# The low halves of the MLPs' turned activations are subtracted by GpSimd, on a semaphore of their own, in place of VectorE

## The chip, the cores and the metric

The kernel runs on one core of one Trainium2 chip. The metric is the time of one execution on the device in microseconds; three runs before the change took 2456.23 to 2458.35, median 2457.49. Durations and starts below come from one profiled execution of that kernel.

Engines by their short names: PE is TensorE (PEld its weight loads), ACT is ScalarE, DVE is VectorE, POOL is GpSimd, SP is SyncE.

## The reference

A trunk of two layers over 256 tokens of width 2048, all in float32: a Mamba-2 mixer and an MLP, then a differential attention over one shared key/value set and a second MLP. What matters here is the MLP, which stands in both layers:

```
h = h + sq_relu_mlp(rms_norm(h, mlp_norm_w[l]), w_up[l], w_down[l])
def sq_relu_mlp(h, w_up, w_down):
    return jnp.square(jax.nn.relu(h @ w_up)) @ w_down      # 2048 -> 8192 -> 2048
```

## The kernel before

**Products in three parts.** A float32 product is made of three matmuls on rounded values: every factor is split into a high half (the value rounded to TensorE's format) and a low half (value minus high half), and TensorE adds high times high, high times low and low times high. ScalarE makes the high halves (a copy that rounds), VectorE the low ones (a subtraction).

**Weights.** They stream from DRAM in pieces of 128x1024 elements (512 KB), 865 of them, through rings of four slots: `raw` (loaded by SyncE), `whi` (ScalarE, `hi`, L741), `wlo` (VectorE, `lo`, L1095). TensorE uses a piece in 12 matmuls (`piece`, L422 to L424) and then raises `w_used`, for which ScalarE's piece four further on waits. So ScalarE and VectorE can be at most four pieces ahead of TensorE. Each engine has its program written out by hand: a loop over the pieces, and at given piece numbers `j`, behind the weight work of this piece, other work.

**An MLP** (`mlp` on each engine) is four chunks of 64 pieces. In a chunk, pieces 0 to 31 multiply by the up weights and give four blocks of 512 hidden columns (u = 0 to 3) in PSUM; pieces 32 to 63 multiply these by the down weights. The second product needs the hidden activations with channels on the partitions, split into halves. For block u this takes:
- `relu` on ScalarE and `square` on VectorE (L1380), then a VectorE transpose within 32x32 squares (`turn`, L1336), which raises `turned`;
- `spread(n)` on GpSimd's queue: one write to DRAM (L1673) and four reads back (L1678) into `channel_tiles`, of which there are two, used by turns. n numbers all blocks that are turned in this way, the MLPs' and the residual stream's: the first MLP's blocks have n = 5 to 20, the second's 29 to 44;
- `up_hi` on ScalarE (L932): waits for the four reads, writes the high half into `st` and raises `turned_hi`;
- `up_lo` on VectorE (L1387): waits for `turned_hi`, writes the low half and raises `turned_lo`.

TensorE waits for `turned_lo` at the first uses of each block among the down pieces (from piece 32 on; block 3 from piece 44). `spread(n)` waits for the low half of block n - 2 before it overwrites that channel tile. The residual stream's blocks go the same way with `resid_hi` and `resid_lo`, and raise the same `turned_lo`.

**Where it stands in the stream.** Tables give, for each block, the last piece of its product, the piece at which it is read (relu, square, transpose, GpSimd's trip) and the piece at which its halves are made. `UPS` holds for the second to fourth chunk, `UPS_FIRST` for the first chunk of each MLP, where blocks 0 and 1 take turns and so end two pieces apart:

```
UPS = ((0, 7, 11, 18), (1, 15, 19, 26), (2, 23, 27, 34), (3, 31, 35, 42))
UPS_FIRST = ((0, 13, 17, 24), (1, 15, 19, 27), (2, 23, 27, 34), (3, 31, 35, 42))
```

At piece 27 of a first chunk ScalarE's order is: high half of the weight piece, `up_hi` of block 1, `relu` of block 2, and then the high half of piece 28. VectorE's is: low half of piece 27, `up_lo` of block 1, square and transpose of block 2, low half of piece 28.

GpSimd has little else in the MLPs: it goes through `spread(n)` for n = 1, 2, 3 ... in order.

Of the kernel before, what the change touches and what calls it, by code (L numbers as in the profile page):

```python
# [17 lines left out]
F32 = mybir.dt.float32  # L18
F32R = mybir.dt.float32r
ALU = mybir.AluOpType  # L20
# [36 lines left out]
T_OUT, T_MLP0, T_MLP0_END, T_WO, T_MLP1 = 0, 4, 20, 24, 28  # L57
# [47 lines left out]
class Chain:  # L105
# [25 lines left out]
    def leave(self, rounds):  # L131
        assert self.n == self.per, (self.n, self.per)
        self.base, self.n = 0, self.before + rounds * self.per


def wait(eng, sem, n):
    if not (isinstance(n, int) and n <= 0):
        eng.wait_ge(sem, n)
# [24 lines left out]
def trunk(nc, x, mlp_norm_w, w_up, w_down, ssm_norm_w, ssm_w_in, ssm_conv_w, ssm_conv_b, ssm_dt_bias,  # L163
# [3 lines left out]
    with ctx:  # L167
# [5 lines left out]
        def sem(name):  # L173
            if name not in sems:
                sems[name] = ctx.enter_context(nc.semaphore(name))
            return sems[name]
# [4 lines left out]
        st = sb("stationary", [P, 3 * KT, 2, SEQ], F32R)  # L181
        RA, RB, RC = 0, KT, 2 * KT
# [104 lines left out]
        channel_tiles = [b.rearrange("p (b k i) -> p k b i", k=4, i=32) for b in channels]  # L287
# [109 lines left out]
        def _(pe):  # L397
# [191 lines left out]
            def mlp(base, R, T, U):  # L589

                def up(c, fresh):
                    for i, (u, kt) in enumerate(WO_ORDER if fresh else PLAIN):
                        if kt == 0:
                            pe.wait_ge(sem("resid_added"), R + 4 * c + u - 3 if c else R if u >= 2 else R - 1)
                        if fresh and u == 0 and kt % 4 == 0:
                            pe.wait_ge(sem("turned_lo"), T - 3 + kt // 4)
                        piece(Pos(base, c, PER_CHUNK), i, banks[u], NB, RA + kt, kt == 0, kt == KT - 2)

                def down(c):
                    for i, (d, kt) in enumerate(WO_ORDER):  # L600
                        if kt == 0:
                            pe.wait_ge(sem("up_read"), c * 4 + (U + d + 1))
                        if d == 0 and kt % 4 == 0:
                            pe.wait_ge(sem("turned_lo"), c * 4 + (T + 1 + kt // 4))
                        if base == UP1 and c == 3 and i == 31:
                            last_piece(Pos(base, c, PER_CHUNK), 32 + i, banks[d], RB + kt)
                        else:
                            piece(Pos(base, c, PER_CHUNK), 32 + i, banks[d], NB, RB + kt, kt == 0, kt == KT - 2)

                for c in range(4):  # L610
                    up(c, c == 0)
                    down(c)
# [48 lines left out]
            def pair(j, first):  # L661
                pos = Pos(ATT0, j, PER_PAIR)
                for i in range(PER_PAIR):
                    m, kt = LATE_ORDER[i] if first else (i // 8, 2 * (i % 8))
                    if first:
                        if i == 0:
                            pe.wait_ge(sem("resid_added"), R_WO - 1)
                        if m == 0 and kt == 12:
                            pe.wait_ge(sem("kv_lo"), 1)
                        elif m == 0 and kt % 4 == 0 or m == 2 and kt == 12:  # L670
                            pe.wait_ge(sem("turned_lo"), T_MLP0_END + 1 + kt // 4)
                    else:
                        if i == 0:
                            wait(pe, sem("o_lo"), j - 1)
                        if i == 8:
                            pe.wait_ge(sem("k_read"), j)
                        if i == 16:
                            pe.wait_ge(sem("q_read"), j)
                    ps, region = ((aux[0], RA), (acc[0], RA), (acc[1], RC))[m]
                    piece(pos, i, ps, NB, region + kt, kt == 0, kt == KT - 2)  # L680
                    if not first:
                        if i == 4:
                            turn_q(j - 1)
                        if i == 7:
                            scores_a(j - 1)
                        if i == 9:
                            pe.wait_ge(sem("v_read"), j + 1)
                            scores_b(j - 1)
                        if i == 15:
                            turn_p(j - 1)  # L690
                        if i == 16:
                            apply_p(j - 1)
                        if i == 20:
                            turn_o(j - 1)
# [393 lines left out]
        def _(v):  # L1088
# [287 lines left out]
            def mlp(base, R, T, U, T_carry, before, after, prev, squared):  # L1376
                def square(c, u):

                    v.wait_ge(sem("relu_made"), c * 4 + (U + u + 1))
                    v.scalar_tensor_tensor(act, banks[u][:, :, :], 0.0, act, ALU.max, ALU.mult).then_inc(sem("up_read"), 1)  # L1380
                    v.wait_ge(sem("up_read"), c * 4 + (U + u + 1))
                    turn(act, c * 4 + (T + u + 1), (T + u + 1) % 2)

                def up_lo(c, u):
                    v.wait_ge(sem("turned_hi"), c * 4 + (T + u + 1))
                    hi, lo = (st[:, RB + 4 * u:RB + 4 * u + 4, i, :].rearrange("p k (b i) -> p k b i", i=32) for i in range(2))
                    v.tensor_tensor(lo, channel_tiles[(T + u + 1) % 2], hi.bitcast(F32), ALU.subtract).then_inc(sem("turned_lo"), 1)  # L1387

                def chunk(c, first, carry):
                    for j in range(PER_CHUNK):  # L1390
                        lo(Pos(base, c, PER_CHUNK), j)
                        if first:
                            if j == 2:
                                resid_lo(2, T - 1, before)
                            if j == 3:
                                prev()
                                turn_resid(3, R, T)
                            if j == 10:
                                resid_lo(3, T, before)
                            if j == 9:  # L1400

                                link(resid_ms(squared))
                                link(v.reciprocal(h_rs, h_ms))
                        elif j == 3:
                            add_resid(3, Pos(base, c, PER_CHUNK), -1, True, banks[3])
                        for u, last, at_read, at_lo in UPS_FIRST if first else UPS:
                            if j == at_read:
                                square(c, u)
                            if j == at_lo:
                                up_lo(c, u)  # L1410
                        for d, last, at_add, at_lo in DOWNS:
                            if j == at_add:
                                add_resid(d, Pos(base, c, PER_CHUNK), last, True, banks[d])
                                if carry:
                                    turn_resid(d, R + 13 + d, T_carry + d + 1)
                            if j == at_lo and carry:
                                resid_lo(d, T_carry + d + 1, after)

                chunk(0, True, False)
                with v.Fori(1, 3) as c:  # L1420
                    chunk(c, False, False)
                chunk(3, False, after is not None)
# [140 lines left out]
        def _(gp):  # L1563
# [104 lines left out]
            def spread(n):  # L1668

                gp.wait_ge(sem("turned"), n)  # L1670
                wait(gp, sem("spread"), (n - 2) * 64)
                scratch = spread_dram[n % 2]
                gp.dma_start(scratch.rearrange("t b c q f -> (b c) t (q f)"),  # L1673
                             squares_t[n % 2].rearrange("p (t f) -> p t f", t=TT)).then_inc(sem("spread_out"), 16)
                gp.wait_ge(sem("spread_out"), n * 16)
                wait(gp, sem("turned_lo"), n - 2)
                for q in range(4):
                    gp.dma_start(channels[n % 2][32 * q:32 * q + 32, :].rearrange("c (b f) -> c b f", f=P),  # L1678
                                 scratch[:, :, :, q, :].rearrange("t b c f -> c (t b) f")).then_inc(sem("spread"), 16)


            gp.wait_ge(sem("resid_added"), 1)
# [5 lines left out]
            gp.wait_ge(sem("masks_made"), 1)  # L1688
            for n in range(1, T_WO + 1):
                spread(n)  # L1690
            gp.wait_ge(sem("h_ms"), 1)
            rsqrt(h_rs, h_ms, "h_rstd")

# [25 lines left out]
            rsqrt(o_rs, o_ss, "o_rstd")  # L1719
            for n in range(T_WO + 1, T_MLP1 + 16 + 1):  # L1720
                spread(n)


# [20 lines left out]
```

## Time and profile before

| | |
|---|---|
| runs, us | 2456.23, 2457.49, 2458.35 |
| span of the profiled execution, us | 2456.4 |
| TensorE busy | 2441.9 us, 99% |
| VectorE busy | 1539.9 us, 63% |
| ScalarE busy | 1195.5 us, 49% |
| GpSimd busy | 259.1 us, 11% |
| chain that ended last | TensorE 99%, DMA 1% |
| granted TensorE clock | 9 tenths or more in all 40 slices |

The profiled execution's own time is not listed apart from its span; the median of the runs is 1.1 us above it. Busy shares are averages over the span. In a timeline a row gives the start, the length, the engine, the line and the operation, then how long the engine had been idle and who ended that.

### The profile page before, as it was taken

Reading aid. Unit: us, or ns where it says so; the run is one execution under the profiler, and the core shown is the slowest. Engines: PE = TensorE matmul, PEld = TensorE weight load, DVE = VectorE, ACT = ScalarE, POOL = GpSimd, SP = SyncE. Lnnn points to the kernel's source line nnn. Section 1 sums busy time; section 2 is a strip of 40 time slices with the busy share of each in tenths; the row PEclk is TensorE's granted clock in tenths of the full one; section 3 lists DMA queues with packets and bytes.
Section 4 is the critical chain, followed back from the end, with each engine's and each line's share of the span. In section 5 each row is a group of like instructions: output and inputs, shape, how many; then the busy total and the mean of one; then the engine's idle time right before and its main releaser. Section 6 shows DMA issues by size and latency. Waiting matters only on the chain.

```text
span 2456.4 us, 32498 instructions
## 1 busy us (share of the span) xinstructions
PE 2441.9 (99%) x11683; PEld 2039.3 (83%) x11683; DVE 1539.9 (63%) x1664; ACT 1195.5 (49%) x1442; POOL 259.1 (11%) x394
## 2 busy tenths in 40 slices
PE   8999999999999999999999999999999999999999
PEld 7888888888888888888888888888888888888887
DVE  5788888875565555565555766666655565565554
ACT  5556555654444344344444545555544444444443
POOL 1011111111011000010011111110110010010010
PEclk9999999999999999999999999999999999999999
DMA  7777777777678677677687766655886686786785
GB/s 205 225 225 228 230 223 228 224 222 238 216 230 241 193 228 230 191 233 223 193 245 238 235 202 194 187 176 175 262 244 213 204 237 207 210 240 197 219 237 169
DMA packets 288103, 535.30 MB, mean 218 GB/s; under 512 B 22318, under 2 KB 55440, under 8 KB 286976
## 3 DMA queue, kind: packets, MB, share of 16 engines
q1 hardware_dynamic: 264736, 457.87, 61.3%
q0 software_dynamic: 22976, 75.91, 11.2%
q8 instruction: 69, 1.13, 0.2%
q14 instruction: 34, 0.28, 0.0%
q10 hardware_dynamic: 288, 0.11, 0.0%
HBM read 498.09 MB, written 35.72 MB: 217 GB/s over the span
## 4 chain that ended last, share of the span: by engine, by line
PE 99%; DMA 1%; DVE 0%; ACT 0%; SPq 0%; issue 0%; ACTq 0%
PE acc L422 18%; PE acc L424 18%; PE acc L423 18%; PE aux L424 12%; PE aux L423 12%; PE aux L422 12%; PE aux L438 1%; PE aux L439 1%; PE aux L437 1%; PE aux L510 1%; PE aux L452 1%; DMA resid<-in_x 1%; PE acc L504 0%; PE aux L653 0%; PE aux L654 0%; PE aux L560 0%
## 5 line engine op out<-in xcount | busy, mean ns | idle before, releaser
L1095 DVE TENSOR_TENSOR w_lo<-w_raw,w_hi 128x1024 fp32r<-128x1024 f32 x865 | 1053.5, 1222 | 824.6 <-ACT w_hi L741 824.0
L741 ACT ACTIVATE w_hi<-w_raw 128x1024 fp32r<-128x1024 f32 x865 | 913.2, 1060 | 1076.9 <-PE acc L424 545.6
L422 PE MATMUL acc<-w_hi,stationary 128*128 128x512 f32 x1984 | 778.5, 392 | 0.0
L424 PE MATMUL acc<-w_hi,stationary 128*128 128x512 f32 x1984 | 773.2, 390 | 0.0
L423 PE MATMUL acc<-w_lo,stationary 128*128 128x512 f32 x1984 | 773.0, 390 | 0.0
L422 PE MATMUL aux<-w_hi,stationary 128*128 128x512 f32 x1340 | 522.1, 390 | 0.0
L424 PE MATMUL aux<-w_hi,stationary 128*128 128x512 f32 x1340 | 521.9, 389 | 0.0
L423 PE MATMUL aux<-w_lo,stationary 128*128 128x512 f32 x1340 | 521.8, 389 | 0.0
L424 PEld LDWEIGHTS acc<-w_hi,stationary 128*128 128x128 f32 x1984 | 372.5, 188 | 77.9
L422 PEld LDWEIGHTS acc<-w_hi,stationary 128*128 128x128 f32 x1984 | 372.6, 188 | 76.4
L423 PEld LDWEIGHTS acc<-w_lo,stationary 128*128 128x128 f32 x1984 | 372.7, 188 | 75.9
L423 PEld LDWEIGHTS aux<-w_lo,stationary 128*128 128x128 f32 x1340 | 251.6, 188 | 52.2
L424 PEld LDWEIGHTS aux<-w_hi,stationary 128*128 128x128 f32 x1340 | 251.6, 188 | 52.1
L422 PEld LDWEIGHTS aux<-w_hi,stationary 128*128 128x128 f32 x1340 | 251.6, 188 | 52.0
L1673 POOL DMA_DIRECT2D spread<-work x44 | 31.8, 723 | 1179.4 <-DVE work L1336 971.9
L1678 POOL DMA_DIRECT2D work<-spread x176 | 102.2, 587 | 169.0 <-DMA spread<-work 164.0
L1575 POOL TENSOR_TENSOR small<-small 128x2 f32<-128x2 f32 (+2 forms) x22 | 43.9, 2001 | 391.7 <-DVE small L1105 391.7
L437 PE MATMUL aux<-stationary,w_hi 128*128 128x256 f32 x256 | 72.6, 284 | 0.0
L439 PE MATMUL aux<-stationary,w_hi 128*128 128x256 f32 x256 | 72.6, 283 | 0.0
L438 PE MATMUL aux<-stationary,w_lo 128*128 128x256 f32 x256 | 72.5, 283 | 0.0
L437 PEld LDWEIGHTS aux<-stationary,w_hi 128*128 128x128 f32 x256 | 49.2, 192 | 0.3
L438 PEld LDWEIGHTS aux<-stationary,w_lo 128*128 128x128 f32 x256 | 49.1, 192 | 0.3
(206 smaller groups left out, 1170.3 us busy)
## 6 DMA issues: line engine op xcount, KB each, us to landing
w_raw<-in_w_up SPq DMA_DIRECT2D x256, 512.0 KB
w_raw<-in_w_down SPq DMA_DIRECT2D x256, 512.0 KB
w_raw<-in_ssm_w_in SPq DMA_DIRECT2D x129, 512.0 KB
w_raw<-in_ssm_w_out SPq DMA_DIRECT2D x64, 512.0 KB
w_raw<-in_w_kv SPq DMA_DIRECT2D x64, 512.0 KB
spread<-work POOLq DMA_DIRECT2D x44, 512.0 KB, 3.8
work<-spread POOLq DMA_DIRECT2D x176, 128.0 KB, 5.0
w_raw<-in_ssm_w_in SPq DMA_DIRECT2D x64, 256.0 KB
```

What stands on the lines that cost most here:

```text
L422: pe.matmul(o, xh, hi[:, k], start=start, stop=False)
L423: pe.matmul(o, xh, lo[:, k], start=False, stop=False)
L424: mm = pe.matmul(o, xl, hi[:, k], start=False, stop=stop)
L437: pe.matmul(o, hi[:, k, i], xh, start=start, stop=False)
L438: pe.matmul(o, lo[:, k, i], xh, start=False, stop=False)
L439: mm = pe.matmul(o, hi[:, k, i], xl, start=False, stop=stop)
L452: tr = pe.transpose(dst(i, t), src(i, t), ident[:, :])
L741: a.activation(whi[:, s, :], raw[:, s, :], ACT.Copy).then_inc(sem("hi_made"), 1)
L1095: v.tensor_tensor(wlo[:, s, :], raw[:, s, :], whi[:, s, :].bitcast(F32), ALU.subtract).then_inc(sem("lo_made"), 1)
L1575: gp.tensor_tensor(out, in_, nhalf[:, 0:out.shape[1]], ALU.pow).then_inc(sem(signal), 1)
L1673: gp.dma_start(scratch.rearrange("t b c q f -> (b c) t (q f)"), squares_t[n % 2].rearrange("p (t f) -> p t f", t=TT)).then_inc(sem("spread ...
L1678: gp.dma_start(channels[n % 2][32 * q:32 * q + 32, :].rearrange("c (b f) -> c b f", f=P), scratch[:, :, :, q, :].rearrange("t b c f -> c ( ...
```

## The change

The subtraction `up_lo` leaves VectorE's program and comes into GpSimd's, with the same operands and shape. It stands behind `spread(n)` for each n that is a block of an MLP, and waits there for `turned_hi`. It raises a new semaphore, `up_lo`, for which TensorE waits in the down product. `turned_lo` now counts the residual's blocks alone, and the numbers waited for are converted by two small functions. Before a channel tile is overwritten, `spread` waits for whichever of the two semaphores belongs to block n - 2.

```diff
+def is_up(n):
+    return T_MLP0 < n <= T_MLP0_END or n > T_MLP1
+def resid_block(n):
+    return n if n <= T_MLP0 else n - 16
+def up_block(n):
+    return n - T_MLP0 if n <= T_MLP0_END else n - T_MLP1 + 16
...
                         if d == 0 and kt % 4 == 0:
-                            pe.wait_ge(sem("turned_lo"), c * 4 + (T + 1 + kt // 4))
+                            pe.wait_ge(sem("up_lo"), c * 4 + (U + 1 + kt // 4))
...
-                def up_lo(c, u):
-                    v.wait_ge(sem("turned_hi"), c * 4 + (T + u + 1))
-                    hi, lo = (st[:, RB + 4 * u:RB + 4 * u + 4, i, :].rearrange("p k (b i) -> p k b i", i=32) for i in range(2))
-                    v.tensor_tensor(lo, channel_tiles[(T + u + 1) % 2], hi.bitcast(F32), ALU.subtract).then_inc(sem("turned_lo"), 1)
...
-                            if j == at_lo:
-                                up_lo(c, u)
...
                 gp.wait_ge(sem("spread_out"), n * 16)
-                wait(gp, sem("turned_lo"), n - 2)
+                if is_up(n - 2):
+                    gp.wait_ge(sem("up_lo"), up_block(n - 2))
+                else:
+                    wait(gp, sem("turned_lo"), resid_block(n - 2))
...
+            def up_lo(n):
+                u = (up_block(n) - 1) % 4
+                hi, lo = (st[:, RB + 4 * u:RB + 4 * u + 4, i, :].rearrange("p k (b i) -> p k b i", i=32) for i in range(2))
+                gp.wait_ge(sem("turned_hi"), n)
+                gp.tensor_tensor(lo, channel_tiles[n % 2], hi.bitcast(F32), ALU.subtract).then_inc(sem("up_lo"), 1)
...
             for n in range(1, T_WO + 1):
                 spread(n)
+                if is_up(n):
+                    up_lo(n)
```

The order on GpSimd at blocks 0 and 1 of the first MLP's first chunk, before: a write and four reads for each block.

```order
L1673 DMA spread<-work 128x2x512 [waits spread,turned]
L1678 DMA work<-spread 32x8x128 [waits turned_lo,spread_out]
L1678 DMA work<-spread 32x8x128 x3
L1673 DMA spread<-work 128x2x512 [waits spread,turned]
L1678 DMA work<-spread 32x8x128 [waits turned_lo,spread_out]
```

And the same place in the changed kernel, whose lines are numbered anew (L1681 is the write, L1689 the reads, L1697 the subtraction):

```order
L1681 DMA spread<-work 128x2x512 [waits spread,turned]
L1689 DMA work<-spread 32x8x128 [waits turned_lo,spread_out]
L1689 DMA work<-spread 32x8x128 x3
L1697 TENSOR_TENSOR stationary<-work,stationary 128x4x256 [waits turned_hi]
L1681 DMA spread<-work 128x2x512 [waits spread,turned]
L1689 DMA work<-spread 32x8x128 [waits turned_lo,spread_out]
```

Between the last read of a block and the write of the next there now stands an operation that waits for ScalarE's `turned_hi`.

VectorE from the transpose of block 1 to that of block 2 in the same chunk, before (L1380 is the square, L1336 the transpose, L1095 the low half of a weight piece, L1387 the subtraction):

```order
L1336 STREAM_TRANSPOSE work<-work 128x2x4x4x32 [waits spread_out,up_read]
L1095 TENSOR_TENSOR w_lo<-w_raw,w_hi 128x1024 [waits hi_made] x5
L1387 TENSOR_TENSOR stationary<-work,stationary 128x4x256 [waits turned_hi]
L1095 TENSOR_TENSOR w_lo<-w_raw,w_hi 128x1024 [waits hi_made] x3
L1387 TENSOR_TENSOR stationary<-work,stationary 128x4x256 [waits turned_hi]
L1380 SCALAR_TENSOR_TENSOR work<-aux,work 128x1024 [waits relu_made]
L1336 STREAM_TRANSPOSE work<-work 128x2x4x4x32 [waits spread_out,up_read]
```

And in the changed kernel:

```order
L1351 STREAM_TRANSPOSE work<-work 128x2x4x4x32 [waits spread_out,up_read]
L1110 TENSOR_TENSOR w_lo<-w_raw,w_hi 128x1024 [waits hi_made] x8
L1395 SCALAR_TENSOR_TENSOR work<-aux,work 128x1024 [waits relu_made]
L1351 STREAM_TRANSPOSE work<-work 128x2x4x4x32 [waits spread_out,up_read]
L1110 TENSOR_TENSOR w_lo<-w_raw,w_hi 128x1024 [waits hi_made] x8
```

The two subtractions are gone from between the weight pieces; the rest stands as it stood. The orders of ScalarE and TensorE have the same instructions at the same places.

## Rows read from the trace of the kernel before

**Rows 1.** The page: busy time by engine, and the chain that ended last.
```profile
PE 2441.9 (99%) x11683; PEld 2039.3 (83%) x11683; DVE 1539.9 (63%) x1664; ACT 1195.5 (49%) x1442; POOL 259.1 (11%) x394
...
PE 99%; DMA 1%; DVE 0%; ACT 0%; SPq 0%; issue 0%; ACTq 0%
```

**Rows 2.** Timeline of TensorE at the start: start, length, engine, operation, idle before.
```profile
15.09 1.97 PE L452 MATMUL aux<-ident,resid 128*128 128x128 f32 x8 [6.41 <-DMA resid<-in_x]
...
19.79 0.28 PE L473 MATMUL acc<-stationary,w_hi 128*64 128x256 f32 x1
```

**Rows 3.** Timeline of VectorE, first MLP, first chunk, pieces 24 and 28.
```profile
739.07 1.23 DVE L1095 TENSOR_TENSOR w_lo<-w_raw,w_hi 128x1024 fp32r<-128x1024 f32 x1 [1.49 <-ACT w_hi L741]
...
749.50 1.22 DVE L1380 SCALAR_TENSOR_TENSOR work<-aux,work 128x1024 f32<-128x1024 f32 x1
750.76 1.25 DVE L1336 STREAM_TRANSPOSE work<-work 128x1024 f32<-128x1024 f32 x1
751.93 2.32 DVE L1095 TENSOR_TENSOR w_lo<-w_raw,w_hi 128x1024 fp32r<-128x1024 f32 x2
```

**Rows 4.** Timeline of ScalarE there: high halves of blocks 0, 1, relu of 2.
```profile
738.94 1.04 ACT L932 ACTIVATE stationary<-work 128x1024 fp32r<-128x1024 f32 x1
...
747.10 1.04 ACT L932 ACTIVATE stationary<-work 128x1024 fp32r<-128x1024 f32 x1
748.05 1.00 ACT L928 ACTIVATE work<-aux 128x1024 f32<-128x1024 f32 x1
```

**Rows 5.** Timeline of TensorE: first matmuls of pieces 27 and 28.
```profile
754.03 0.39 PE L422 MATMUL aux<-w_hi,stationary 128*128 128x512 f32 x1
...
756.75 0.39 PE L422 MATMUL aux<-w_hi,stationary 128*128 128x512 f32 x1
```

**Rows 6.** Groups by line and shape: busy time, mean ns, idle before.
```profile
L1387 DVE TENSOR_TENSOR stationary<-work,stationary 128x1024 fp32r<-128x1024 f32 x32 | 39.0, 1219 | 2.2 <-ACT stationary L932 2.2
...
L1568 POOL TENSOR_SCALAR_AFFINE_SELECT work<-work 128x256 f32<-128x256 f32 x8 | 7.0, 876 | 9.9 <-ACT work L860 9.9
```

**Rows 7.** Timeline of VectorE and GpSimd in the mixer, from 128 us.
```profile
128.15 2.29 DVE L1304 TENSOR_TENSOR work<-work,colv 128x2048 f32<-128x2048 f32 x1
...
128.33 2.68 POOL L1575 TENSOR_TENSOR small<-small 128x2 f32<-128x2 f32 x1 [14.39 <-DVE small L1105]
```

**Rows 8.** Timeline, first MLP, second chunk: ScalarE's block 0, GpSimd's block 1.
```profile
896.64 1.05 ACT L932 ACTIVATE stationary<-work 128x1024 fp32r<-128x1024 f32 x1
...
903.52 0.72 POOL L1673 DMA_DIRECT2D spread<-work  x1 [15.52 <-DVE work L1336]
```

**Rows 9.** Timeline of GpSimd, first chunk: write of block 1, trip of block 2.
```profile
730.27 0.72 POOL L1673 DMA_DIRECT2D spread<-work  x1
...
752.30 0.72 POOL L1673 DMA_DIRECT2D spread<-work  x1 [12.64 <-DVE work L1336]
756.36 2.33 POOL L1678 DMA_DIRECT2D work<-spread  x4 [3.34 <-DMA spread<-work]
```

**Rows 10.** L1678's landings for the four copies from 727.96, 1367.52 and 1855.66.
```profile
DMA to landing us min/median/max: 3.7/3.8/5.4
...
DMA to landing us min/median/max: 3.2/3.3/3.6
...
DMA to landing us min/median/max: 4.1/4.8/7.9
```

**Rows 11.** Timeline of GpSimd and ScalarE, second MLP, first chunk, block 3.
```profile
1855.66 2.32 POOL L1678 DMA_DIRECT2D work<-spread  x4 [5.35 <-DMA spread<-work]
...
1865.30 1.06 ACT L932 ACTIVATE stationary<-work 128x1024 fp32r<-128x1024 f32 x1 [1.23 <-DMA work<-spread]
```

**Rows 12.** Timeline of ScalarE, second MLP, first chunk: high halves of blocks 0, 1.
```profile
1815.01 1.04 ACT L932 ACTIVATE stationary<-work 128x1024 fp32r<-128x1024 f32 x1
...
1823.17 1.05 ACT L932 ACTIVATE stationary<-work 128x1024 fp32r<-128x1024 f32 x1
```

**Rows 13.** The chain in order of time: eight later transposes.
```profile
70.52 0.87 PE aux L452 x8
```

More of the change, by code:

```diff
@@ L595, in up @@
                         if fresh and u == 0 and kt % 4 == 0:
-                            pe.wait_ge(sem("turned_lo"), T - 3 + kt // 4)
+                            pe.wait_ge(sem("turned_lo"), resid_block(T - 3) + kt // 4)
                         piece(Pos(base, c, PER_CHUNK), i, banks[u], NB, RA + kt, kt == 0, kt == KT - 2)
@@ L670, in pair @@
                         elif m == 0 and kt % 4 == 0 or m == 2 and kt == 12:
-                            pe.wait_ge(sem("turned_lo"), T_MLP0_END + 1 + kt // 4)
+                            pe.wait_ge(sem("turned_lo"), resid_block(T_MLP0_END + 1) + kt // 4)
                     else:
@@ L1721, in _ @@
                 spread(n)
+                if is_up(n):
+                    up_lo(n)
 _INS = ["x", "mlp_norm_w", "w_up", "w_down", "ssm_norm_w", "ssm_w_in", "ssm_conv_w", "ssm_conv_b", "ssm_dt_bias",
```

## The prediction

> **What bounds the kernel now.** I read the page first. TensorE is busy for 2441.9 of 2456.4 us, the chain that ended last is TensorE for 99%, and the other engines have room: VectorE 63%, ScalarE 49%, GpSimd 11% [rows 1]. TensorE's one long wait lies at the start, 6.41 us for the input [rows 2]. So work taken from VectorE can give nothing by itself: no matmul waits for it. What can move the time is a wait that the change creates and that reaches TensorE. For that I read the timelines of ScalarE, VectorE, GpSimd and TensorE side by side, where the subtractions stand.
>
> The pipeline: each weight piece goes ScalarE (high half, L741), VectorE (low half, L1095), TensorE (12 matmuls; piece 27 starts at 754.03 and piece 28 at 756.75, so 2.72 us a piece [rows 5]). The ring has four slots, so the halves of a piece are ready well before use. Piece 24 of the first MLP's first chunk had its low half at 739.07 + 1.23 = 740.30 [rows 3], and was begun four pieces before 756.75, at 745.87: a cover of 5.6 us. Piece 28 is the tight one. Behind piece 27 ScalarE makes the high half of block 1 (747.10) and the relu of block 2 (748.05) [rows 4]; VectorE then squares, transposes (749.50, 750.76) and only then makes the low half of piece 28, 751.93 + 1.16 = 753.1 [rows 3]. TensorE wants it at 756.75 [rows 5]. The cover there is 3.65 us.
>
> **The change part by part.**
> (a) Removed: 32 VectorE subtractions of 1219 ns, 39.0 us [rows 6]. Worth nothing, since what hides them is the matmul stream itself (99%). The one place where it shortens a path is just behind ScalarE's op at 747.10: the square no longer stands behind the subtraction and can follow the relu at once, 0.4 us earlier than now.
> (b) Added: 32 GpSimd subtractions of the same size. The trace has none on this engine. Lower bound: what VectorE needs, 1.2 us. Upper bound: GpSimd's AFFINE_SELECT over a quarter of the elements took 876 ns, so four times that, 3.5 us [rows 6]. The two ends are far apart and neither row is nearer in kind (one has the operation, the other the engine), so I take the middle, 2.4 us. The Trainium skill (GPSIMD Engine Reference, "3.1 Elementwise — side-by-side cycle accounting") gives 4497 ns for a two-input fp32 operation of 2048 elements, so an estimate of 2.25 us for 1024; no run here shows it yet, and by it each stall below would be 0.15 us shorter.
> (c) GpSimd's operation may wait for VectorE. At 128.33 a GpSimd operation on two columns took 2.68 us, just as long as it took until 0.57 us behind the end of a VectorE operation of 2.29 us with two inputs in SBUF, begun 0.18 us before it [rows 7]. In the first chunk ScalarE's block ends at 738.94 + 1.04 = 739.98 while the subtraction of piece 24 runs until 740.30 [rows 3, 4]: I start GpSimd at 740.3. The Trainium skill (SBUF — State Buffer, "Who interferes with whom") says that a VectorE instruction with two SBUF inputs and a GpSimd instruction that reads SBUF exclude each other for the whole instruction; the trace agrees so far (2.68 us). It speaks against the change: by it each of the 32 also holds up a weight subtraction by up to its own length. With no exclusion GpSimd would start 0.3 us earlier. Held up by 2.4 us, a weight subtraction stays inside the 5.6 us of cover, so this costs nothing more.
> (d) Moved, and this decides: the subtraction sits in GpSimd's single stream between one block's four copies back and the next block's trip through DRAM. GpSimd waits in it for the high half of block n; queued behind it are the next block's one write and four reads, then the next subtraction; for them ScalarE waits, and behind ScalarE the weight pieces. In an ordinary chunk that is free: the high half ends at 896.64 + 1.05 = 897.7, and the next trip starts at 903.52 anyway [rows 8], so the subtraction has 5.8 us. In the first chunk of each MLP it is not: blocks 0 and 1 are ready two pieces apart, so block 1's trip was issued at 730.27 [rows 9], 8.7 us before block 0's high half even began.
>
> The sum for that place:
> - subtraction 740.3 to 742.7; the trip of block 1 issued at 742.75 in place of 730.27.
> - first copy back 4.06 us later (752.30 to 756.36 [rows 9]), at 746.8; the fourth follows after three issues of 0.58, at 748.55 (four take 2.32).
> - the fourth copy is the last to land. Of three trips the slowest copy landed after 5.4, 3.6 and 7.9 us [rows 10]; that of the third is the fourth copy (1855.66 + 1.74 + 7.9 = 1865.30, where ScalarE had waited for it [rows 11]). I take 6.2, somewhat above the middle of the ends, since the weight loads compete until the ring is full and then stop. It lands at 754.75 instead of in time for 747.10.
> - from there the chain of (ScalarE block 0.95, relu 1.00, hand-over 0.1, square 1.26, transpose 1.17, low half of piece 28 1.16) is 5.65 us: ready at 760.4.
> - needed at 756.75: TensorE stands still for 3.65 us.
>
> The second MLP has the same spacing: high halves at 1815.01 and 1823.17, 8.16 us apart, as 738.94 and 747.10 [rows 4, 12]. So two stalls, 7.3 us. Block 2's trip then starts near 759.5 in place of 752.30 and would hold ScalarE some 2 us more at piece 34, but there is no relu behind it and the 5.6 us of cover hold. The low halves themselves are used from piece 32 on (767.6) and are done by 742.7; the last is wanted at piece 44, some 8 us behind its end. Everything later shifts with TensorE.
>
> The span becomes 2456.4 + 7.3 = 2463.7 us. The median of the runs shown, 2457.49, lies 1.1 us above that span, so I add it: 2464.8, given as 2465.
>
> **The rivals.**
> 1. Not slower: the copies land fast enough. The mechanism is the same trip, with a subtraction of 1.2 us and a last landing of 3.6 us [rows 6, 10]: issued at 741.55, last copy begun at 747.35, landed at 750.95, piece 28 ready at 756.6, just before 756.75. It decides from there: subtraction and landing together up to 5.0 us. For it: when ScalarE stops, the ring fills and the weight loads stop too, which leaves the queues to these copies. Against it: only one of the three rows is that short. The time is then 2457.5; a half-way form (landing 4.5, subtraction 2.2) gives 1.75 us a stall and 2461.
> 2. The stalls also cost clock. After the idle 6.41 us at the start, eight transposes took 1.97 us where eight later ones took 0.87, and the slow pace ended by the matmul at 19.79 [rows 2, 13]. That is the lower of the two levels, 1.2 GHz, for 4.7 us of work, 2.3 us lost. For it: a standstill of 3.65 us. Against: the shown idle was nearly twice as long, and the granted clock is 2.4 GHz in all 40 slices of the page. It would give 2465 + 2 x 2.3 = 2469.5.
> 3. A GpSimd subtraction much longer than its upper bound: from 5.8 us on it also delays the trips of the 24 ordinary blocks. Against: the longest GpSimd operation among the rows, held up for most of it, is 2.68 us [rows 7]. At 6 us the two stalls are 7.25 us each, so 2472.
> 4. The change does not do what it says: faster, because VectorE's 39 us come back. The chain has no VectorE share for it to come back from.
>
> **How the numbers follow.** Forecast 0.52, rival 1 0.24, rival 2 0.16, rival 3 0.07, rival 4 0.01. The ends of the unknown costs: 1.2 and 3.6 give no stall, 2457.5; 3.5 and 7.9 give 3.65 + 1.1 + 1.7 = 6.45 each, 2470.4, and with the clock 2475. The range 2457.5 to 2472 leaves out the upper corner of rivals 2 and 3. The forecast's own range, with landings from 5 to 7.5, is 2461 to 2469. About 0.2%, 4.9 us, is what a measurement of this kernel tells from no change, so a stall must be above 2.45 us to count: that holds for most of the forecast, for rivals 2 and 3, and for little of rival 1. Slower 0.70, same 0.28, faster 0.02.
>
> **What would show it.** In the new profile: TensorE waits for the low half (w_lo) twice, once in each MLP, 27 to 28 pieces into its first chunk, 2 to 5 us each, and ScalarE waits just before it for a DMA of work from spread, about 7 us. The write of block 1 is issued right behind the GpSimd subtraction, some 4 us after the start of ScalarE's block 0 in place of 8.7 us before it. In ordinary chunks the writes start when the transposes end, as now, and nobody waits. If TensorE waits nowhere, the landing was the wrong term; if it waits in every chunk, the length of the subtraction was.

## The result, and the profile after

| | before | changed |
|---|---|---|
| median of 5 runs, us | 2457.39 | 2465.79 |
| lowest to highest | 2456.18 to 2458.35 | 2463.84 to 2468.64 |
| ratio (95% interval) | | 1.0038 (1.0026 to 1.0051) |
| span of the profiled execution | 2456.4 | 2465.7 |

The change makes the kernel slower by 0.38% by the ratio; the medians lie 8.4 us apart, 0.34%. A time of 2465 was predicted, 7.3 us of it loss. The profiled execution of the changed kernel took 1.7 us more than the median of its runs, so the two spans lie 9.3 us apart and not 8.4. In what follows a trip is the write of one block to DRAM and its four copies back, and a landing is the time from the issue of a copy to its arrival.

The page of the changed kernel, busy time and the chain that ended last (before: [rows 1]):

```profile
PE 2443.9 (99%) x11683; PEld 2038.8 (83%) x11683; DVE 1527.4 (62%) x1632; ACT 1194.4 (48%) x1442; POOL 338.5 (14%) x426
...
PE 87%; issue 6%; DMA 3%; DVE 2%; ACT 1%; POOL 1%; SPq 0%; DVEq 0%; ACTq 0%; POOLq 0%
```

TensorE's busy time hardly moves, but the chain now leaves it. GpSimd gained 79.4 us. VectorE lost only 12.5 of the 39.0 us taken from it. Groups of instructions by line say why (busy time, mean ns, idle before): the weight subtractions before and after, and GpSimd's new operation (VectorE's before: [rows 6]):

```profile
L1095 DVE TENSOR_TENSOR w_lo<-w_raw,w_hi 128x1024 fp32r<-128x1024 f32 x865 | 1053.5, 1222 | 824.6 <-ACT w_hi L741 824.0
```
```profile
L1110 DVE TENSOR_TENSOR w_lo<-w_raw,w_hi 128x1024 fp32r<-128x1024 f32 x865 | 1076.7, 1251 | 833.5 <-ACT w_hi L756 832.6
```
```profile
L1697 POOL TENSOR_TENSOR stationary<-work,stationary 128x1024 fp32r<-128x1024 f32 x32 | 79.0, 2468 | 284.3 <-ACT stationary L947 284.3
```

One subtraction takes 2468 ns on GpSimd against 1219 on VectorE, and the weight subtractions grew by 23.2 us in all; the 3.3 us that are left of the 26.5 lie in VectorE's other lines. The one that meets the first GpSimd subtraction is in VectorE's timeline below with 1.87 us.

TensorE's waits, in total (waited for, times, longest):

```profile
PE aux L437 <- DVE w_lo L1110: 7.8, 2, 4.8
```

Two waits for a weight's low half that were not there. They stand where they were expected, and the timelines show how they come about. First MLP, GpSimd (before: [rows 9]):

```profile
739.52 2.50 POOL L1697 TENSOR_TENSOR stationary<-work,stationary 128x1024 fp32r<-128x1024 f32 x1 [9.82 <-ACT stationary L947]
741.98 0.73 POOL L1681 DMA_DIRECT2D spread<-work  x1
745.73 2.33 POOL L1689 DMA_DIRECT2D work<-spread  x4 [3.02 <-DMA spread<-work]
```

ScalarE (before: [rows 4]):

```profile
738.39 1.05 ACT L947 ACTIVATE stationary<-work 128x1024 fp32r<-128x1024 f32 x1
...
753.68 1.06 ACT L947 ACTIVATE stationary<-work 128x1024 fp32r<-128x1024 f32 x1 [7.04 <-DMA work<-spread]
```

VectorE and TensorE (before: [rows 3, 5]):

```profile
741.24 1.87 DVE L1110 TENSOR_TENSOR w_lo<-w_raw,w_hi 128x1024 fp32r<-128x1024 f32 x1 [1.50 <-ACT w_hi L756]
...
758.11 4.59 DVE L1110 TENSOR_TENSOR w_lo<-w_raw,w_hi 128x1024 fp32r<-128x1024 f32 x4
```
```profile
759.35 0.50 PE L437 MATMUL aux<-w_hi,stationary 128*128 128x512 f32 x1 [2.98 <-DVE w_lo L1110]
```

Read downwards: GpSimd idle for 9.82 us until the high half of block 0 is there; its subtraction; the write of block 1 right behind; the copies; ScalarE idle for 7.04 us; the four low halves made in a burst once it goes on; TensorE idle for 2.98 us. In the second MLP the same happens with larger numbers, and a new one. GpSimd and ScalarE:

```profile
1821.38 0.73 POOL L1681 DMA_DIRECT2D spread<-work  x1
1826.95 2.33 POOL L1689 DMA_DIRECT2D work<-spread  x4 [4.85 <-DMA spread<-work]
```
```profile
1834.94 1.06 ACT L947 ACTIVATE stationary<-work 128x1024 fp32r<-128x1024 f32 x1 [8.89 <-DMA work<-spread]
```

TensorE there, the stretch behind its wait, and for comparison the stretch behind the wait of the first MLP (columns of the second and third fence: stretch, length, busy time with count of PE, PEld, DVE, ACT and POOL, granted clock, DMA share, GB/s):

```profile
1840.61 0.79 PE L437 MATMUL aux<-w_hi,stationary 128*128 128x512 f32 x1 [4.83 <-DVE w_lo L1110]
...
1842.06 0.63 PE L437 MATMUL aux<-w_hi,stationary 128*128 128x512 f32 x1
1842.48 0.63 PE L438 MATMUL aux<-w_lo,stationary 128*128 128x512 f32 x1
```
```profile
1840.60:1843.30 2.70, 2.69 (x6) 2.15 (x7) 2.70 (x3) 0.09 (x1) 0.00 (x0) 0.50 0.84 227
```
```profile
759.30:763.00 3.70, 3.65 (x16) 2.99 (x17) 3.40 (x3) 0.13 (x1) 0.43 (x1) 1.00 0.87 237
```

The write took 5.57 us to the first copy here, 3.75 in the first MLP, although it was issued at the same place between two weight loads both times (SyncE issued the next load at 743.13 and at 1822.55, 1.15 and 1.17 us behind the write). And behind this wait the clock was granted at 0.50, its level of 1.2 GHz: six matmuls follow each other at 0.43 us and more in place of 0.227 (2.72 us for the 12 of a piece), which costs about 1.4 us. Behind the first wait it stayed at 2.4 GHz.

Stalls of 7.8 and clock of 1.4 make 9.2 of the 9.3 us between the two spans. The agreement to 0.1 us is partly chance: before the first stall this execution was 0.55 us ahead of the other (ScalarE's block 0 at 738.39 against 738.94).

An ordinary chunk is as it was (before: [rows 8]): the subtraction ends at 903.03, the next write starts at 906.93 when VectorE has turned the block.

```profile
900.54 2.49 POOL L1697 TENSOR_TENSOR stationary<-work,stationary 128x1024 fp32r<-128x1024 f32 x1 [9.71 <-ACT stationary L947]
906.93 0.73 POOL L1681 DMA_DIRECT2D spread<-work  x1 [3.90 <-DVE work L1351]
```

### The profile page after: what moved, and what is told of

Same layout as the page of the kernel before. It is cut to its first block, busy times and chain, and to the rows that moved or that the text cites. A ratio compares the mean times of both kernels' runs of the same rounds, so it can differ in the third digit from the quotient of the medians.

```text
span 2465.7 us, 32482 instructions
## 1 busy us (share of the span) xinstructions
PE 2443.9 (99%) x11683; PEld 2038.8 (83%) x11683; DVE 1527.4 (62%) x1632; ACT 1194.4 (48%) x1442; POOL 338.5 (14%) x426
## 4 chain that ended last, share of the span: by engine, by line
PE 87%; issue 6%; DMA 3%; DVE 2%; ACT 1%; POOL 1%; SPq 0%; DVEq 0%; ACTq 0%; POOLq 0%
PE acc L437 16%; PE acc L439 16%; PE acc L438 16%; PE aux L437 11%; PE aux L439 11%; PE aux L438 11%; DMA spread<-work 1%; PE aux L453 1%; PE aux L454 1%; PE aux L452 1%; DVE w_lo L1110 1%; DMA work<-back 1%; PE aux L525 1%; PE aux L467 1%; POOL work L1689 0%
## 5 line engine op out<-in xcount | busy, mean ns | idle before, releaser
L1110 DVE TENSOR_TENSOR w_lo<-w_raw,w_hi 128x1024 fp32r<-128x1024 f32 x865 | 1076.7, 1251 | 833.5 <-ACT w_hi L756 832.6
L1681 POOL DMA_DIRECT2D spread<-work x44 | 32.0, 727 | 845.2 <-DVE work L1351 661.2
L1689 POOL DMA_DIRECT2D work<-spread x176 | 102.4, 588 | 162.0 <-DMA spread<-work 157.0
L1697 POOL TENSOR_TENSOR stationary<-work,stationary 128x1024 fp32r<-128x1024 f32 x32 | 79.0, 2468 | 284.3 <-ACT stationary L947 284.3
```

What stands on the lines that cost most here:

```text
L1110: v.tensor_tensor(wlo[:, s, :], raw[:, s, :], whi[:, s, :].bitcast(F32), ALU.subtract).then_inc(sem("lo_made"), 1)
L1697: gp.tensor_tensor(lo, channel_tiles[n % 2], hi.bitcast(F32), ALU.subtract).then_inc(sem("up_lo"), 1)
```

## The experiments

All are compared with runs of the kernel before on the same chip: experiments 1 to 4 with one set of them (median 2457.70), 5 to 8 with another (2457.42), 9 with a third (2458.04).

| kernel | median us | ratio to before (95%) |
|---|---|---|
| 1 trip of block 1 first | 2457.42 | 1.0000 (0.9991 to 1.0009) |
| 2 bare wait | 2465.70 | 1.0030 (1.0018 to 1.0042) |
| 3 GpSimd in ordinary chunks only | 2458.41 | 1.0001 (0.9992 to 1.0010) |
| 4 GpSimd in first chunks only | 2467.01 | 1.0040 (1.0027 to 1.0054) |
| 5 subtraction made twice | 2475.59 | 1.0074 (1.0060 to 1.0087) |
| 6 halves of block 1 at piece 30 | 2465.90 | 1.0037 (1.0023 to 1.0051) |
| 7 bare wait, light loads | 2457.56 | 1.0003 (0.9994 to 1.0012) |
| 8 changed kernel, light loads | 2461.29 | 1.0016 (1.0007 to 1.0025) |
| 9 halves at 30, and block 2's trip first | 2457.41 | 1.0000 (0.9991 to 1.0009) |

**1. The trip of block 1 ahead of the subtraction of block 0.**

```diff
+FIRST_BLOCKS = (T_MLP0 + 1, T_MLP1 + 1)
                 spread(n)
-                if is_up(n):
+                if is_up(n) and n not in FIRST_BLOCKS:
+                    if n - 1 in FIRST_BLOCKS:
+                        up_lo(n - 1)
                     up_lo(n)
```

> The changed kernel with one thing moved: in the first chunk of each MLP, GpSimd makes the trip of block 1 before it subtracts block 0 (then both subtractions, then block 2); all 32 subtractions stay on GpSimd. Theory A (GpSimd's order: the trip of block 1 stands behind a wait for block 0's high half): both stalls of TensorE vanish, 2457.5 us, ratio 1.000 within 0.001, and ScalarE waits for no copy at piece 27. Rival B (GpSimd's subtractions themselves cost, by holding up VectorE's weight subtractions through the SBUF port): the time stays near 2465, since the same 32 subtractions run. Rival C (block 2's trip, now behind two subtractions, becomes the late one): a smaller stall at piece 34, 2459 to 2461.

Measured: ratio 1.0000, TensorE waits for nothing but its input. GpSimd:

```profile
740.09 2.50 POOL L1700 TENSOR_TENSOR stationary<-work,stationary 128x1024 fp32r<-128x1024 f32 x1 [1.60 <-ACT stationary L950]
747.33 2.52 POOL L1700 TENSOR_TENSOR stationary<-work,stationary 128x1024 fp32r<-128x1024 f32 x1 [4.73 <-ACT stationary L950]
751.00 0.73 POOL L1684 DMA_DIRECT2D spread<-work  x1 [1.16 <-DVE work L1354]
```

All 32 subtractions run on GpSimd at the same 2.5 us, and the weight subtractions take 1251 ns in the mean here too: the whole loss was the order at one place per MLP. Rivals B and C fall.

**2. The bare wait.** VectorE subtracts as before; GpSimd only waits.

```diff
                 spread(n)
+                if T_MLP0 < n <= T_MLP0_END:        # and n > T_MLP1 in the second loop
+                    gp.wait_ge(sem("turned_hi"), n)
```

> The kernel before, with VectorE's subtractions where they were, and a bare wait of GpSimd for the block's high half behind each trip. Theory A (it is the place in the queue): the trip of block 1 is issued at about 739.9 to 740.1 in place of 742.0 in the changed kernel, so each stall is about 2.5 us shorter, less 0.4 us for the subtraction that stands again before the square: 1 us in the first MLP, 1 to 3 in the second, 2459 to 2461.5. Rival B (the cost is GpSimd's operation): no stall, 2457.5.

Measured: 2465.70, above the expected range. Rival B falls, but the size is off: in time the wait alone costs as much as wait and subtraction. GpSimd and ScalarE, first MLP:

```profile
739.68 0.72 POOL L1673 DMA_DIRECT2D spread<-work  x1 [10.00 <-ACT stationary L932]
746.00 2.33 POOL L1678 DMA_DIRECT2D work<-spread  x4 [5.60 <-DMA spread<-work]
```
```profile
753.91 1.06 ACT L932 ACTIVATE stationary<-work 128x1024 fp32r<-128x1024 f32 x1 [7.32 <-DMA work<-spread]
```

The write started 2.3 us earlier than in the changed kernel, and its first copy 0.3 us later: 6.32 us in place of 3.75. The stalls were 3.49 and 2.53 us, 6.0 in place of the 7.8 of the changed kernel, and the clock was at its lower level behind both: 13 matmuls at 0.43 us and more in the first MLP, 8 in the second, where the fall came 1.5 us after TensorE had started again. That costs about 2.8 and 1.6 us, 4.4 in all. So the loss has another make-up than in the changed kernel: less standstill, more clock. The profiled execution took 4.1 us more than the median of its runs, so the median run had less of one or the other. (A third wait, of 0.78 us at 1394.83, lies outside the MLPs.) What lengthened the write is the question of experiments 7 and 8.

**3 and 4. The two halves of the change.** In 3, VectorE makes the eight subtractions of the first chunks and GpSimd the other 24; in 4 it is the other way round. The edit in 3 (in 4 both conditions are turned over):

```diff
+                            if j == at_lo and first:
+                                up_lo(c, u)                # VectorE, raising up_lo
...
-                if is_up(n):
+                if is_up(n) and not in_first(n):
                     up_lo(n)                               # GpSimd
```

> GpSimd subtracts only the 24 blocks of the second to fourth chunks; the 8 blocks of the two first chunks are VectorE's again (on the same new semaphore). Theory A: no stall, 2457.5 us, ratio 1.000 within 0.001, although 24 operations of 2.5 us run on GpSimd and delay weight subtractions by up to 2.5 us. Rival B (exclusion through the port costs in proportion): three quarters of the loss, 2463.7.

> The complement: GpSimd subtracts only the 8 blocks of the two first chunks, VectorE the other 24. Theory A: the whole loss, 2464 to 2467. Rival B: a quarter of it, 2459.5.

Measured: 1.0001 and 1.0040. The loss is wholly in the first chunks. With 24 subtractions on GpSimd the weight subtractions took 1246 ns in the mean in place of 1222, and no loss came of it that these runs tell apart. The profiled execution of experiment 4 is the fastest of its five runs (2464.23): stalls of 2.04 and 3.38 us, and no fall of the clock.

**5. The subtraction made twice.**

```diff
+                link(gp.tensor_tensor(lo, channel_tiles[n % 2], hi.bitcast(F32), ALU.subtract))
                 gp.tensor_tensor(lo, channel_tiles[n % 2], hi.bitcast(F32), ALU.subtract).then_inc(sem("up_lo"), 1)
```

> The changed kernel with each GpSimd subtraction made twice, one behind the other, so that about 5.0 us stand where 2.5 us stood. Theory A (order on GpSimd): the trip of block 1 in each first chunk is issued 2.5 us later, each stall is 2.5 us longer, plus 1.3 us in the first MLP too if the clock falls there as it did in the second MLP of the changed kernel: 2470.5 to 2473. Ordinary chunks stay free, since 5.0 is under the 5.8 us they have. Rival (proportional cost of the exclusion): the loss doubles, 2474.

Measured: 2475.59, above the expected range. GpSimd and TensorE, first MLP:

```profile
742.24 3.27 POOL L1698 TENSOR_TENSOR stationary<-work,stationary 128x1024 fp32r<-128x1024 f32 x1
745.47 0.73 POOL L1681 DMA_DIRECT2D spread<-work  x1
```
```profile
762.52 0.80 PE L437 MATMUL aux<-w_hi,stationary 128*128 128x512 f32 x1 [6.02 <-DVE w_lo L1110]
763.12 0.63 PE L438 MATMUL aux<-w_lo,stationary 128*128 128x512 f32 x1
```

The second subtraction took 3.27 us beside a weight subtraction that had started to wait at 741.38 and ended at 743.24, 1.07 us behind the end of GpSimd's first. Where VectorE had nothing waiting, the second took no longer than the first:

```profile
756.58 2.36 POOL L1697 TENSOR_TENSOR stationary<-work,stationary 128x1024 fp32r<-128x1024 f32 x1 [5.02 <-ACT stationary L947]
759.02 2.36 POOL L1698 TENSOR_TENSOR stationary<-work,stationary 128x1024 fp32r<-128x1024 f32 x1
```

So the trip of block 1 was issued 3.3 to 3.4 us later than in the changed kernel, counted from ScalarE's block 0 (6.94 and 6.93 us behind it, in place of 3.59 and 3.58), where 2.5 was expected. The stalls are 6.02 and 6.40 us, 12.4 in all, 4.6 above the changed kernel. That is near the 5.0 expected, but not by equal steps: 3.0 more in the first MLP, and 1.6 in the second, where the write took 3.81 us in place of 5.57. The rest is clock, which was low behind both stalls and for longer (11 matmuls in the first MLP, 12 in the second), at 2.3 and 2.5 us where I had expected 1.3. TensorE waits for no low half elsewhere, so the ordinary chunks stayed free. The rival, a doubled loss, gave 2474 and lies nearer to the total than theory A's 2473; it is experiments 1 and 3 that rule it out, not this one.

**6. ScalarE comes later for block 1.**

```diff
-UPS_FIRST = ((0, 13, 17, 24), (1, 15, 19, 27), (2, 23, 27, 34), (3, 31, 35, 42))
+UPS_FIRST = ((0, 13, 17, 24), (1, 15, 19, 30), (2, 23, 27, 34), (3, 31, 35, 42))
```

> The changed kernel with one number changed: in the first chunks, block 1's halves are made at piece 30 instead of 27 (ScalarE's table; GpSimd's order stays: subtraction of block 0, then the trip of block 1, which is still late). Theory A's second half (ScalarE waits too early, in front of the weight pieces): the copies land before ScalarE comes to them, no stall at piece 28; block 2's trip is pushed to about 759 and ScalarE waits 2 to 3 us for it at piece 34, inside the cover: 2457.5, at most 2459. Rival (the late trip delays something else too): above 2460.

Measured: 2465.90, no gain. The stall at piece 28 went away, and one at piece 35 came. ScalarE, GpSimd and VectorE there:

```profile
754.77 1.05 ACT L947 ACTIVATE stationary<-work 128x1024 fp32r<-128x1024 f32 x1
...
773.11 1.06 ACT L947 ACTIVATE stationary<-work 128x1024 fp32r<-128x1024 f32 x1 [7.37 <-DMA work<-spread]
```
```profile
755.90 2.50 POOL L1697 TENSOR_TENSOR stationary<-work,stationary 128x1024 fp32r<-128x1024 f32 x1 [7.76 <-ACT stationary L947]
758.35 0.73 POOL L1681 DMA_DIRECT2D spread<-work  x1
764.34 2.33 POOL L1689 DMA_DIRECT2D work<-spread  x4 [5.26 <-DMA spread<-work]
774.25 2.38 POOL L1697 TENSOR_TENSOR stationary<-work,stationary 128x1024 fp32r<-128x1024 f32 x1 [7.59 <-ACT stationary L947]
```
```profile
775.15 2.57 DVE L1110 TENSOR_TENSOR w_lo<-w_raw,w_hi 128x1024 fp32r<-128x1024 f32 x1 [8.15 <-ACT w_hi L756]
```

ScalarE no longer waits for block 1 in the first MLP (754.77, no idle time; 0.95 us in the second). But block 1's subtraction now stands in front of block 2's trip, whose write takes 5.99 us, and ScalarE waits 7.37 us for block 2. Here the exclusion of the two engines lies on the path: VectorE's subtraction takes 2.57 us, 1.3 above its usual, beside GpSimd's (774.25 to 776.63), and TensorE waits 2.30 us for just that one. I had summed the later block with a wait of 2 to 3 us. In the first MLP the write (5.99 us) and the last copy's landing (7.0) made it 7.4; in the second the write took only 3.78 us, but the last copy landed after 8.1, and ScalarE waited 7.19. TensorE stood still for 2.13 us there (until 1857.85), and from 0.9 us later on the clock was at its lower level for 8 matmuls, some 1.5 us lost.

**7 and 8. Lighter weight loads.** Of pieces 28 to 31 of each first chunk only an eighth is loaded, so the products that use the rest of these weights are not the model's.

```diff
+            LIGHT = (28, 29, 30, 31)
+            def light(pos, off, src):
+                wait(sp, sem("lo_made"), pos.done(off) - RING)
+                dst = raw[:, pos.slot(off), :].rearrange("p (k n) -> p k n", k=2)
+                sp.dma_start(dst[:, :, 0:64], src).then_inc(sem(f"raw_in{pos.slot(off)}"), 32)
...
+                            if i in LIGHT:
+                                light(pos, i, up[:, kt:kt + 2, u * NB:u * NB + 64])
```

> The bare-wait kernel with the weight loads of pieces 28 to 31 of each first chunk cut to an eighth (7/8 of these four pieces' weights are left out; instructions and waits stay). In the bare-wait kernel the trip was issued 2.3 us earlier than in the changed one, yet its write took 6.3 us instead of 3.8. Theory D (the write and the weight loads share the DMA engines, and the wait puts the write just where a load starts): the write takes 4 us or less, the last copy lands 5 us or less after its issue, the stalls shrink to 0 to 1 us each: 2457.5 to 2459.5. Rival E (the write is long because of VectorE's subtraction, which starts at the same moment, or for its own reasons): unchanged, 2465.

> The changed kernel with the same four loads of each first chunk cut to an eighth (7/8 of these pieces' weights are left out). Theory D: the write keeps its 3.8 us in the first MLP (it fell between two loads) and gets there from 5.6 in the second; the last copy lands earlier than 6.2 us after its issue; stalls of 1 to 2 us each instead of 3.0 and 4.8, no fall of the clock: 2459.5 to 2461.5. Rival (landing is GpSimd's own cost): 2464 to 2466.

Measured: 2457.56 and 2461.29, both times inside what theory D had. The bare wait with light loads, GpSimd and ScalarE:

```profile
739.33 0.72 POOL L1684 DMA_DIRECT2D spread<-work  x1 [10.05 <-ACT stationary L943]
742.84 2.32 POOL L1689 DMA_DIRECT2D work<-spread  x4 [2.80 <-DMA spread<-work]
```
```profile
747.58 1.06 ACT L943 ACTIVATE stationary<-work 128x1024 fp32r<-128x1024 f32 x1 [1.34 <-DMA work<-spread]
```

The write is down from 6.32 to 3.51 us (in the second MLP from 6.20 to 3.50) with VectorE's subtraction where it was, so rival E falls. The landings of block 1's four copies in the first MLP, in the changed kernel and in it with light loads:

```profile
DMA to landing us min/median/max: 4.4/4.7/6.2
```
```profile
DMA to landing us min/median/max: 2.8/2.9/3.0
```

So about 3 of the 6.2 us that the last copy takes are the weight loads beside it. In the second MLP the last copy's landing falls from 6.2 to 3.4 us. The write there does not follow: theory D had it fall to the 3.8 us of the first MLP, and with light loads it still takes 4.86 (first MLP: 3.69):

```profile
1818.92 0.73 POOL L1692 DMA_DIRECT2D spread<-work  x1
1823.78 2.33 POOL L1700 DMA_DIRECT2D work<-spread  x4 [4.13 <-DMA spread<-work]
```

What makes this one write long is open. The changed kernel with light loads has one wait of 1.14 us left, in the second MLP, and none in the first; 1 to 2 us in each were expected. Its time fits all the same, but the stall in the profile is only 1.1 of the 3.9 us between the medians. The profiled execution took 1.3 us less than the median of its runs, and what the others waited for is not recorded.

**9. Both orders at once.** Experiment 6, and block 2's trip ahead of block 1's subtraction.

```diff
-UPS_FIRST = ((0, 13, 17, 24), (1, 15, 19, 27), (2, 23, 27, 34), (3, 31, 35, 42))
+UPS_FIRST = ((0, 13, 17, 24), (1, 15, 19, 30), (2, 23, 27, 34), (3, 31, 35, 42))
-                if is_up(n):
+                if is_up(n) and n not in SECOND_BLOCKS:
+                    if n - 1 in SECOND_BLOCKS:
+                        up_lo(n - 1)
                     up_lo(n)
```

> The kernel with block 1's halves at piece 30, and in addition GpSimd makes the trip of block 2 before it subtracts block 1 (block 0's subtraction still stands before the trip of block 1, as in the change). In the kernel with the halves at 30 alone the stall had gone from piece 28 to piece 35, because block 2's trip went from 752 to 758 behind block 1's subtraction, took 6.0 us for its write, and ScalarE waited 7.4 us for it. Theory A: both waits are then met by time that is free: block 1's trip at about 742 lands at about 754, just before ScalarE comes to it, block 2's trip is issued at about 751: no stall of TensorE, 2457.5, ratio 1.000 within 0.001. Rival (the two stalls have a cause that the order does not touch, such as the exclusion of the two engines): 2461 to 2466.

Measured: ratio 1.0000, no wait of TensorE behind its input. GpSimd:

```profile
741.74 0.73 POOL L1684 DMA_DIRECT2D spread<-work  x1
745.62 2.33 POOL L1692 DMA_DIRECT2D work<-spread  x4 [3.15 <-DMA spread<-work]
750.38 0.72 POOL L1684 DMA_DIRECT2D spread<-work  x1 [2.43 <-DVE work L1354]
```

The trip of block 1 is as late as in the change, and free, since ScalarE comes three pieces later. Together with experiment 1 this shows the loss as one of order, and that it can be mended on either side of the wait. No version was faster than the kernel before.

## Why the prediction was right

The way was right: a wait of GpSimd in front of a trip, and through ScalarE and VectorE two stalls of TensorE. The time was right to 0.8 us and the loss to 1.1 (7.3 expected, 8.4 between the medians). That it came so near is partly luck: the first stall was 0.7 us shorter and the second 1.2 longer than expected, and in the profiled execution 1.4 us of clock come on top that the sum put at nothing.

- **Nothing to gain from VectorE.** Right: with the order mended (experiments 1 and 9) the kernel stands at 1.0000, though VectorE has 32 subtractions less.
- **Length of the subtraction, 2.4 us taken.** 2.47 measured. The estimate from the Trainium skill (GPSIMD Engine Reference, "3.1 Elementwise — side-by-side cycle accounting"), 2.25 us, was 0.2 us low, and the middle of the two rows nearer.
- **The exclusion of the two engines.** Right in kind: 23.2 us more of weight subtractions on VectorE, hidden, as experiments 1 and 3 show. It reached the path in experiment 5, where it made GpSimd's second subtraction 0.9 us longer, and in experiment 6.
- **Place.** Two stalls at piece 28 of each first chunk, ordinary chunks free: shown by experiments 1, 3 and 4.
- **The trip.** Expected to be issued 3.81 us behind the start of ScalarE's block 0, measured 3.59. Write to first copy 4.06 expected, 3.75 and 5.57 measured. Last copy 6.2 expected, and 6.2 in both MLPs. From ScalarE's restart to piece 28's low half 5.65 expected, 758.11 + 1.16 - 753.68 = 5.59 measured. Block 2's trip was expected near 759.5 with 2 us of waiting at ScalarE, and came at 758.49 with 3.21 us, inside the cover.
- **The stalls.** 3.65 each expected, 2.98 and 4.83 measured: 7.3 against 7.8 in all. The term that was off is the write, which I had taken from one row (4.06 us) and given no range. The kernel before already had longer ones, block 1's of the first MLP with 7.07 us behind the four copies of block 0 (issued at 730.27, [rows 9]) and block 3's of the second with 6.07 [rows 11]:

```profile
737.34 2.32 POOL L1678 DMA_DIRECT2D work<-spread  x4 [6.34 <-DMA spread<-work]
```

Experiments 2 and 7 show it go from 6.3 to 3.5 us when the weight loads beside it are lightened; experiment 8 shows that the loads do not account for all of the 5.57 in the second MLP.

- **The range of the forecast itself.** Landings from 5 to 7.5 us were said to give 2461 to 2469; by the prediction's own sum they give stalls of 2.45 to 4.95 us, so 2462.4 to 2467.4.
- **From span to time.** The 1.1 us added compares a span with a median. In every run that has both, the time is 1.7 to 1.8 us above its own span, so the profiled execution before was some 0.6 us slower than its median.
- **Clock.** I had it as a rival with 0.16. It came true in one of the two stalls of the profiled execution, and costs 1.4 us there, not 2.3. The 9 in all 40 slices of the page, held against it, says little: the page of the changed kernel shows 9 in all 40 as well, for a slice is 62 us. The clock fell behind both stalls in experiments 2 and 5, behind the one in the second MLP in experiment 6, and behind neither in experiment 4. That this is what spreads the changed kernel's runs over 4.8 us, where those of before lie within 2.2, is my reading and not shown: stalls and clock of the runs that were not profiled are not recorded.
- **Rival 1, not slower since the copies land fast.** Experiment 8 shows it at work in the first MLP when the weight loads are light (landing 3.0 us, no stall), so it was a question of the traffic, and the traffic decides against it.

## What to carry to other kernels

Before an operation that waits is put into an engine's stream, ask what is queued behind it and when that was issued until now, at the place where the stream is closest packed and not where it is regular: here 24 of the 32 places lay in ordinary chunks and were free, and of the other 8 it took only two, those behind block 0's copies, to lose 0.38% (experiment 1 moves just these). When an operation moves between a transfer's landing and the next transfer's issue, issue the next transfer first. A wait that is shortened or moved may be given back by the DMA queues or by the next block, so an experiment that removes a suspected term should be read in the timeline and not only in the time.

## What was not expected of the hardware

- A write of 512 KB from GpSimd's queue took 3.5 us to its first copy with light weight loads (experiment 7), and 6.3 us when it was issued within 0.1 us of a load (experiment 2, 739.68 and 739.72). Issued 1.15 us ahead of a load in the changed kernel it took 3.75 us once and 5.57 the other time; what tells the two apart is open. An issue 2.3 us earlier brought nothing.
- The clock fell behind stalls of 2.13 us (experiment 6) and 2.53 us (experiment 2), 0.9 and 1.5 us after TensorE had started again, and not behind one of 2.98 us (changed kernel), nor behind 2.04 and 3.38 us in experiment 4. Behind 6.02 us it stayed low for some 4.5 us of matmuls.
- Of two GpSimd subtractions back to back the second took 3.23 us in the mean, the first 2.47: where VectorE had a subtraction waiting, it went in between, and where it had none the second took 2.36.
